# One program part for a whole decoder layer, and a query projection that does not wait for the norm

## The reference, cut to what matters

```python
def hybrid_mixer(n, ...):
    u = n @ w_in                                   # n = rmsnorm(h, norm_mix_w)
    u_a, u_b, u_c, u_g = jnp.split(u, [A_IN, A_IN + B_IN, A_IN + B_IN + SSD_IN], axis=-1)
    y_a = short_conv_mixer(u_a, conv_a_w) @ w_branch_a       # 3 x 2048 columns
    y_b = stick_breaking_attention(u_b) @ w_branch_b         # 3 x 2048 columns, 16 heads
    y_c = mamba2_ssd(u_c, ...) @ w_branch_c                  # 8 groups, 64 heads, d_skip = ssd_d per head
    g_a, g_b, g_c = jnp.split(jax.nn.sigmoid(u_g), 3, axis=-1)
    return (g_a * y_a + g_b * y_b + g_c * y_c) @ w_out

def peer_ffn(n, w_query, sub_keys, expert_down, expert_up):  # n = rmsnorm(h, norm_ffn_w)
    q = (n @ w_query).reshape(256, 8, 2, 128)
    s = jnp.einsum('thcd,hcnd->thcn', q, sub_keys)
    ...                                            # top 16 x 16 candidates, top 16, softmax gate
    act = jax.nn.gelu(jnp.einsum('td,tkd->tk', n, expert_down[idx]), approximate=False)
    return jnp.einsum('tk,tkd->td', gate * act, expert_up[idx])

h = h + hybrid_mixer(rmsnorm(h, norm_mix_w), ...)
h = h + peer_ffn(rmsnorm(h, norm_ffn_w), ...)
return rmsnorm(h, final_norm_w)
```

## Time and profile before

| | |
|---|---|
| median of 3 runs | 3772.51 us |
| the profiled execution | 3772.85 us |
| its span, first to last instruction | 3771.1 us (1.75 us lie outside) |
| TensorE busy | 3515.0 us (93%) |
| VectorE, ScalarE busy | 59%, 45% |
| mean granted TensorE clock | 0.971 |
| DMA | 57.6% of 16 engines, 164 GB/s |

### The profile page before, as it was taken

How to read it: one execution, slowest core, us unless ns; L and a number is a source line. 1 busy time by engine, 2 the same in 40 slices (tenths; PEclk the granted TensorE clock), 3 DMA queues, 4 the chain that set the end, 5 groups by cost and what they waited for, 6 DMA issues and landing times. The chain is left out here.

```text
span 3771.1 us, 67412 instructions
## 1 busy us (share of the span) xinstructions
PE 3515.0 (93%) x23349; PEld 3236.6 (86%) x23349; DVE 2231.5 (59%) x2615; ACT 1708.8 (45%) x2241; POOL 27.9 (1%) x32
## 2 busy tenths in 40 slices
PE   7998989998959999978998799999999999999997
PEld 7997889987859999976887799989999988888886
DVE  4554434444416677663444499988888965555554
ACT  3333335453314555543333334435777744444443
POOL 0000000000000000000000000000000000000000
PEclk9999999998969999988999899999999999999999
DMA  5555545536435454415645566666666667766665
GB/s 172 178 176 164 192 150 158 155 107 201 156 88 166 144 154 147 142 59 192 198 145 201 145 157 171 162 153 175 160 158 160 159 185 193 192 194 194 192 193 183
DMA packets 463970, 619.33 MB, mean 164 GB/s; under 512 B 60176, under 2 KB 322656, under 8 KB 462432
## 3 DMA queue, kind: packets, MB, share of 16 engines
q1 hardware_dynamic: 463840, 617.56, 57.6%
HBM read 613.15 MB, written 4.19 MB: 164 GB/s over the span
## 5 line engine op out<-in xcount | busy, mean ns | idle before, releaser
L114 PE MATMUL bank<-xT_hi,w_hi 128*128 128x256 f32 x2304 | 665.7, 289 | 34.3 <-DVE w_lo L1758 23.6
L115 PE MATMUL bank<-xT_lo,w_hi 128*128 128x256 f32 x2304 | 653.1, 283 | 0.0
L116 PE MATMUL bank<-xT_hi,w_lo 128*128 128x256 f32 x2304 | 653.0, 283 | 0.0
L1824 DVE TENSOR_TENSOR w_lo<-w_raw,w_hi 128x1024 fp32r<-128x1024 f32 x256 | 313.7, 1225 | 337.5 <-PE bank L116 337.0
L114 PEld LDWEIGHTS bank<-xT_hi,w_hi 128*128 128x128 f32 x2304 | 442.9, 192 | 46.0 <-DVE w_lo L1758 30.9
L115 PEld LDWEIGHTS bank<-xT_lo,w_hi 128*128 128x128 f32 x2304 | 443.3, 192 | 0.0
L116 PEld LDWEIGHTS bank<-xT_hi,w_lo 128*128 128x128 f32 x2304 | 442.8, 192 | 0.0
L114 PE MATMUL bank<-w_hi,u_coef_hi 128*128 128x512 f32 x1024 | 398.4, 389 | 0.0
L115 PE MATMUL bank<-w_lo,u_coef_hi 128*128 128x512 f32 x1024 | 398.3, 389 | 0.0
L116 PE MATMUL bank<-w_hi,u_coef_lo 128*128 128x512 f32 x1024 | 398.3, 389 | 0.0
L114 PE MATMUL bank<-xT_hi,c_hi 128*128 128x256 f32 x1280 | 370.4, 289 | 24.6 <-DVE c_lo L104 23.4
(11 more groups left out here) (309 smaller groups left out, 7444.6 us busy)
## 6 DMA issues: line engine op xcount, KB each, us to landing
w_raw<-in_peer_down SPq DMA_DIRECT2D x1024, 128.0 KB, 3.5
w_raw<-in_peer_up SPq DMA_DIRECT2D x1024, 128.0 KB, 2.7
c_raw<-in_w_in SPq DMA_DIRECT2D x256, 256.0 KB, 2.9
a_raw<-in_w_in SPq DMA_DIRECT2D x192, 256.0 KB, 3.0
b_raw<-in_w_in SPq DMA_DIRECT2D x192, 256.0 KB, 3.1
gc_raw<-in_w_branch_c SPq DMA_DIRECT2D x64, 512.0 KB, 4.7
ga_raw<-in_w_in SPq DMA_DIRECT2D x32, 512.0 KB, 4.6
ga_raw<-in_w_branch_a SPq DMA_DIRECT2D x32, 512.0 KB, 4.8
```

The costliest lines, as they stand in the source:

```text
L114: nc.tensor.matmul(out, lhs[0], rhs[0], start=start, stop=False, skip_group_check=True)
L115: nc.tensor.matmul(out, lhs[0], rhs[1], start=False, stop=False, skip_group_check=True)
L116: return nc.tensor.matmul(out, lhs[1], rhs[0], start=False, stop=stop, skip_group_check=True)
L1824: v.tensor_tensor(lo[u % 2][:, :], raw[u % NR][:, :], hi[u % 3][:, :].bitcast(F32), ALU.subtract).then_inc(lo_done, 1)
```

## The change

The whole kernel becomes one block. One ring of buffers (`Flow`: 4 raw, 2 hi, 2 lo of 1280 columns, one count of units for all stages) takes the place of the streams from a to o, so that loads and splits of the next stage are issued while the stage before still runs. What the last iteration of a stage left to do is issued within the next stage (`ga_hook`, `gb_hook`, `gc_hook`).

- Units in a and b are 768 columns (one k row block, 16 an iteration), loaded by 4 DMAs of 32 partitions; b now has 2 hi buffers. Units in ga, gb, gc and o are 1024 columns (12 matmuls of 512), unrolled, with gate and branch segments in the order `ORDER` over changing pairs of banks.
- The dt block runs inside ga as `dt_step`; its products are 48 of 256 columns. Its loads, `d_col` among them, are issued on SP behind the loads of iteration 0 of a.
- The transposes for o stand in gc; the 16 keys' transposes stand in o.
- The query projection takes h times the norm's weight (`xU`, 32 transposes of h more). The factor per token multiplies the scores when they are copied. The normalised rows, which e needs, are made and transposed inside q.
- h is written to `h_scratch` behind the first 8 query units and read back, with the final norm's weight, after 40 of the 64 load groups of u. The end runs in halves of 1024 columns.

The diff, cut to its core:

```diff
-        class Stream:
-            def __init__(self, ctx, tag, cols, units, pieces, split=2):
+        class Flow:
+            def __init__(self):
+                self.raw = [place(f"f_raw{i}", [P, SLOT // 4], at_ring + i * SLOT) for i in range(4)]
+                self.hi = [place(f"f_hi{i}", [P, SLOT // 4], at_ring + (4 + i) * SLOT, F32R) for i in range(2)]
+                self.lo = [place(f"f_lo{i}", [P, SLOT // 4], at_ring + (6 + i) * SLOT, F32R) for i in range(2)]
...
+            def room(self, sp, n):
+                if not (isinstance(n, int) and n < 4):
+                    sp.wait_ge(self.lo_done, n - 3)
...
+                def ab_load(n, col, it, u):
+                    fl.room(sp, n)
+                    for q in range(4):
+                        sp.dma_start(fl.raw[u % 4][32 * q:32 * q + 32, 0:W_AB].rearrange("p (i n) -> p i n", i=3),
+                                     w_in[0, u * P + 32 * q:u * P + 32 * q + 32, col:col + 3 * D].rearrange(
+                                         "r (i n) -> r i n", i=3)[:, :, ds(it * 256, 256)]).then_inc(fl.raw_full[u % 4], 16)
...
+                for u in range(U_AB):
+                    ab_load(u, COL_A, 0, u)
+                sp.dma_start(w_raw[:, :].rearrange("p (k n) -> p k n", k=KD),
+                             w_in[0, :, COL_DT:COL_DT + P].rearrange("(k p) n -> p k n", p=P)).then_inc(d_w, 16)
...
+                heads = ssd_d.rearrange("o (c h) -> h (o c)", h=2)
+                for h in range(2):
+                    sp.dma_start(d_col[64 * h:64 * h + 64, :], heads[h:h + 1, :].to_broadcast([64, KC]),
+                                 allow_slow_non_contiguous=True).then_inc(d_vec, 16)
+                with sp.Fori(1, N_AB) as it:
+                    for u in range(U_AB):
+                        ab_load(U_AB * it + u, COL_A, it, u)
+                branch_load(GA0, COL_G, w_branch_a, KD)
...
+                with act.Fori(1, N_AB) as it:
+                    for u in range(U_AB):
+                        fl.split_hi(act, B0 + U_AB * it + u, B0 // 4 + 4 * it, u, W_AB)
+                        if u == 0:
+                            copy_qk(it - 1)
+                        if u == 6:
+                            softplus(it - 1)
+                        if u == 12:
+                            weights_b(it - 1)
+                        if u == 15:
+                            o_hi_b(it - 1)
...
                     for tb in range(TB):
                         act.wait_ge(q_s, 2 * it + tb + 1)
                         nc.scalar.activation(scores[:, tb, 4 * it:4 * it + 4, :],
                                              bank[4 + tb][:, :].rearrange("p (k n) -> p k n", k=4),
-                                             ACT.Copy).then_inc(q_sc, 1)
+                                             ACT.Copy, scale=f_rstd[:, tb:tb + 1]).then_inc(q_sc, 1)
...
+                with sp.Fori(0, 40) as it:
+                    u_load(it)
+                sp.wait_ge(u_lo, 60)
+                for tb in range(TB):
+                    sp.dma_start(z_h[:, tb, :], h_dram[tb * P:(tb + 1) * P, :]).then_inc(z_in, 16)
+                sp.dma_start(wide[:, :], final_norm_w.rearrange("(o d) -> o d", o=1).to_broadcast([P, D])).then_inc(z_in, 16)
```

More of the change, by code:

```diff
@@ L42 @@
 V_SSDN = 320
+V_QUERY = 352
 NEG = -30000.0
@@ L66, in program @@
         ident = sb(top, "ident", [P, P])
-        vcols = sb(top, "vcols", [P, 352])
-        spare = sb(top, "spare", [P, 32])
+        vcols = sb(top, "vcols", [P, 368])
+        spare = sb(top, "spare", [P, 16])
         eps_col = sb(top, "eps_col", [P, 1])
-        class Stream:
-            def __init__(self, ctx, tag, cols, units, pieces, split=2):
[L77 to L109, removed]
         def tri_matmul(out, lhs, rhs, start, stop):
@@ L1363, in program, with ends @@
+        def ends(kb):
+            out, m = [], 0
+            for kind, p in ORDER:
+                m += 8 if kind == "g" else kb // 2
+                out.append(m)
+            return out
         NR, QU, EU, UU = 4, 32, 256, 256
@@ new lines, in _ @@
+                dve.wait_ge(b_const, 9)
+                for u in range(U_AB):
+                    fl.split_lo(dve, B0 + u, u, W_AB)
+                    if u == 1:
+                        gate("ga", GA0, KD, 3, GA_PAIRS[7])
+                with dve.Fori(1, N_AB) as it:
+                    for u in range(U_AB):
+                        fl.split_lo(dve, B0 + U_AB * it + u, u, W_AB)
+                        if u == 0:
+                            copy_v(it - 1)
+                        if u == 7:
+                            softplus(it - 1)
+                        if u == 12:
+                            exponent(it - 1)
+                        if u == 15:
+                            o_lo_b(it - 1)
@@ new lines, in query_turn @@
+                def query_turn(p):
+                    pe.wait_ge(o_h, TB * p + TB)
+                    for pair in (2 * p, 2 * p + 1):
+                        if pair < 2:
+                            pe.wait_ge(o_lo, KD)
+                        else:
+                            pe.wait_ge(x_lo_done, 2 * pair - 2)
+                        for k in (2 * pair, 2 * pair + 1):
+                            for tb in range(TB):
+                                at = (k % 2) * T + tb * P
+                                last = nc.tensor.transpose(O_TR[pair % 2][:, at:at + P],
+                                                           acc[:, tb, k * P:(k + 1) * P], ident[:, :])
+                            last.then_inc(x_tr, 1)
@@ L1904, in scatter, with down_turn @@
                     last.then_inc(m_mm, 1)
+                def down_turn(pair):
+                    pe.wait_ge(f_scaled, 2)
+                    if pair < 2:
+                        pe.wait_ge(f_kc, 4)
+                    else:
+                        pe.wait_ge(f_lo, 2 * pair - 2)
+                    for k in (2 * pair, 2 * pair + 1):
+                        for tb in range(TB):
+                            at = (k % 2) * T + tb * P
+                            last = nc.tensor.transpose(bank[6 + pair % 2][:, at:at + P],
+                                                       hn[:, tb, k * P:(k + 1) * P], ident[:, :])
+                        last.then_inc(f_tr, 1)
                 for it in range(4):
+                    if it == 1:
+                        pe.wait_ge(o_h, 4 * TB)
+                        pe.wait_ge(x_lo_done, KD)
                     if it >= 2:
```

2544 lines of the change are left out of this document (1314 added, 1230 removed).

## The result

The changed kernel takes 3659.95 us (median of 4 runs, 3657.51 to 3664.55), the kernel before in the same comparison 3772.09 us. The ratio is 0.9705, 95% interval 0.9688 to 0.9722: 112 us less, where 81 were forecast. 3659.95 lies in the range of 3640 to 3735.

A forecast was written before the change was run, and what follows sets the result against it. TensorE was busy 93% of the span, leaving about 256 us to win. Savings 184.5 + 5, less 44, 39, 11, 9.5 and 5, gave 81 off 3772.85: 3691 us, range 3640 to 3735.

The forecast's parts named there:

- mechanism of the boundaries: Stage changes: waits at a stage's first product go; a-ga +16, ga-b +10.4, b-gb +18, gb-c +60, c-gc +40, o-q +15.
- d_col loads: In a, between units 15 and 16: 4-byte elements hold SP's queue, TensorE stands about 42 us and starts cold: -44.
- Rival 1: In a: the d_col loads do not hold the queue, later loads pass; 3647 us, chance 0.20.
- Iterations of a: Loop of a: no wait for its copies any more, 0.68 us in each of 7 iterations: +5.
- first product: Start of a: first product at about 19 us instead of 33.4, less 5 us for splits in iteration 0: +9.
- line as a whole: Start to the last product of a: forecast +9 for the start, +5 for the loop, -44 for d_col.
- b: a size: Softplus and weights in b delay copies: 5.5 us in each of 7 iterations, -39 in all.
- rival 4: Table loads between copies, as in b, each add a drain of 1.38 us; 3713 us, chance 0.03.
- o to q: Between o and q: norm, write of h and barrier leave the path, 31 us; half taken: +15.
- rival 2: SyncE's issues become the bound: 3732 us at 0.56 us an issue, chance 0.08; beyond 0.60, chance 0.04.
- price at 0.50: SyncE in a and b: at 0.50 us an issue a unit needs 2.0 and 0.1 for its wait, under 2.17.
- u and the end: In u, 3 MB of loads ahead of weights cost -5; the end's chain of 20.5 us shortens, +9.

The follow-up runs named there:

- e1: Changed kernel with ssd_d loaded as whole rows in one DMA and laid out by two small VectorE copies in ga: 3622.08 us.
- e2: Changed kernel with the two d_col loads issued twice, the second pair into a scratch tile: 3700.26 us.
- e3: Changed kernel with the two d_col loads issued by GpSimd on its own queue instead of SP's: 3662.85 us.
- e7: Changed kernel with the two d_col loads issued by ACT on its own hardware queue: 3656.07 us in one run.
- e4: Changed kernel with 4 instead of 2 hi buffers in a and b, lo staying at 2: 3625.84 us.
- e6: Changed kernel with the query projection waiting for the norm again, in one program part: 3661.7 us; again, beside the changed kernel (3661.3) on one chip, 3670.3 us.

## Why the prediction was right, and where it was off

**The mechanism of the boundaries** held to a few us in five of six places; each is a row of the table. Most of the prize came from the reading that those waits occur once, at a stage's first product.

**The d_col loads** did what the profile before allowed one to foresee. The line that loads them, after:

```profile
L487 SPq DMA_DIRECT2D d_col<-in_ssd_d x2: 659/2298/3937, 51.0 to 51.7; - x2
...
DMA to landing us min/median/max: 22.0/31.6/41.1
```

They land at 73.1 and 92.9, 19.8 us apart, where the earlier trace rows have 18.4 (the 19.1 between the two durations leaves out that the second is issued 0.7 later). SP's timeline has them ahead of the loads of iteration 1:

```profile
47.95 0.43 SPq L479 DMA_DIRECT2D dt_w_raw<-in_w_in  x1
48.43 1.95 SPq L481 DMA_DIRECT2D dt_bias<-in_ssd_dt_bias  x1
50.42 0.59 SPq L483 DMA_DIRECT2D dt_a_log<-in_ssd_a_log  x1
51.05 4.64 SPq L487 DMA_DIRECT2D d_col<-in_ssd_d  x2
```

The hole runs from 56.75 to 96.61: 39.9 us where 42 were forecast. Behind it the products start 0.21 us apart again, as in the earlier trace rows. Rival 1 is refuted by e1 and e2. The reason given, SP's order, is only half: e3 and e7 show that the elements hold the weights from each of the three queues. What spoke for rival 1, a DMA share of 0.18 while such elements move, was read as room for other transfers; with a share of 4.7% there was none.

**Iterations of a** did not lose their 0.68 us: the wait for `a_c` (0.69, six times) stands as before, since it comes from two copies of the banks and not from the stream. I had it down as a wait that goes (+5). The loop lost 0.4 us an iteration instead, for the chain of copy, rest and weights that is as long as the unit; e4 takes it back. The first product came at 19.13 us as forecast, and less of it was given back in iteration 0 than the 5 us, so the line as a whole came out at -31.5 against -30: errors that cancel, and partly luck.

**b: a size.** The term said 5.5 us an iteration (3.8 at the softplus, 1.7 at the weights); it is 4.0. The timeline of ACT at the place that the earlier trace rows shows:

```profile
626.58 0.84 ACT L122 ACTIVATE f_hi<-f_raw 128x768 fp32r<-128x768 f32 x1 [1.34 <-PE bank L80]
630.05 0.84 ACT L122 ACTIVATE f_hi<-f_raw 128x768 fp32r<-128x768 f32 x1 [2.62 <-PE bank L80]
630.80 0.85 ACT L643 ACTIVATE b_z_abs<-bank 128x384 f32<-128x384 f32 x2
631.68 0.84 ACT L645 ACTIVATE b_z_exp<-b_z_abs 128x768 f32<-128x768 f32 x1
632.54 1.28 ACT L647 ACT_TABLE_LOAD   x1
633.84 0.84 ACT L647 ACTIVATE b_z_ln<-b_z_exp 128x768 f32<-128x768 f32 x1
634.59 1.56 ACT L122 ACTIVATE f_hi<-f_raw 128x768 fp32r<-128x768 f32 x2
```

The group takes the 3.8 us, but the copy after it could not have started at once: in the unit's rhythm ACT waits 1.34 us for a buffer before each copy (first row). That slack comes off. TensorE waits 2.11 and 0.32 us here and 1.11 at the weights, 3.5 in all; the wait for `b_q` (0.69) comes on top, as one for `b_k` did before. All its waits of an iteration are 4.2 us against 1.2, and it is busy 0.9 us longer, which makes the 4.0. Taking the group's length for the hole ignored what ACT would have idled anyway. Copies of 768 columns took 0.84 to 0.85 us and the rests 0.96, as estimated. The table load is followed by ln after 0.02 us here too, so rival 4 is out. (An iteration has three table loads and not the two that the prediction counts: a third stands before the loop's first copy.)

**o to q: the step that failed.** "Given back: 32 more transposes, their copies on ACT and DVE, and the normalised rows made inside q and crowding against the first choice of experts, on a DVE that is near its limit in e. I take half: +15." Nothing was given back here: the piece is 32.7 us shorter, the whole of the 30 us between the stages and 2.6 more. (24 of the 32 transposes stand in o, whose piece shows no loss either, 44.9 against 42.5.) TensorE's waits for e's `lo` are 21.1 us in 46 times after and were 23.6 in 48 before: no crowding. The half was not worked out from any row. It should have been the sum of parts as elsewhere: what DVE does more in q lies beside it, with DVE idle over a quarter of the 103 us from 2012 on (74 busy). e6 gives the share of the query's order alone: 9 of these 32.7 us, 13 by its first comparison. The other 20 to 24 come without it, from one program part. Ten of them can be named from the waits before, for the keys, whose load and transposes no longer stand there:

```profile
PE bank L1348 <- DMA f_keys<-in_peer_sub_keys: 10.1, 1, 10.1
```

The write of h off the path and the loads and splits of q done ahead are the likely rest; they were not taken apart.

**SyncE (rival 2)** did not decide. In a the issues of a unit start 0.50 us apart as in u, and at least 0.56 lie between the last of a unit and the next one's first: 2.06 us a unit, where a unit of TensorE takes 2.24. So the price at 0.50 was the right one. SyncE's recorded waits are 8.3 us in the 180 from 134.9 on; it was some 8% from being the bound. In e4 it does 64 issues in 35.22 us, with TensorE busy for 34.54 of them.

**u and the end** were right: 3.0 us of wait at 3380.8 (forecast 5), and the end 11.8 us long. VectorE's two results of 1024 columns now end it, without a read or a table load:

```profile
3648.28 2.48 DVE L1645 SCALAR_TENSOR_TENSOR z_result<-z_h,z_rstd,z_wide 128x1024 f32<-128x1024 f32 x2
...
3651.39 2.48 DVE L1645 SCALAR_TENSOR_TENSOR z_result<-z_h,z_rstd,z_wide 128x1024 f32<-128x1024 f32 x2
```

Of the 33 us by which the time was missed, 18 are the step from o to q, 12 the size in b, the rest small. The saved parts of the forecast add up to 184.4, not 184.5, which changes nothing.

## What to carry to other kernels

When separate parts are joined into one stream, look first at what used to stand in the gaps: a transfer of a few KB in 4-byte pieces that cost 19 us beside a barrier costs the same 19 us in the middle of a weight stream, from each of the three queues tried. A DMA share near zero is no sign that the queue is free. Halving a unit halves the time that a ring of the same depth covers; a group of work on the copying engine then shows, less the idle time which that engine would have had in any case. Where a forecast says "half", it has not been worked out.

## What the hardware showed that was not expected

Two transfers of 2048 elements of 4 bytes make TensorE wait 39.9 us for weights when issued by SyncE, 39.4 by GpSimd and 36.6 by ACT (one run). In the first case the 16 DMA engines are busy for 4.7% of the 33 us in the middle of that wait, and the issue of the next load takes 18.9 us instead of 0.32. The same 64 numbers as 128 rows of 256 bytes landed in 4.7 us beside the stream, with no wait of TensorE over 2.1 us.
